# A second attention in thirteen phases beside a streaming projection, its second round moved behind a layer norm

## What is computed

```python
h = rms_norm(x, mix_norm_g)
q, kv, gate_logits, conv_in = split(h @ w_in_2)
gates = sigmoid(gate_logits)               # one for each head and branch
# three attentions: over 15 compressed blocks, over chosen blocks, over a window
p_cmp = masked_softmax(q @ k_cmp + bias_c); o_cmp = p_cmp @ v_cmp
p_sel = masked_softmax(q @ k_slc + bias_s); o_sel = p_sel @ v_slc
p_win = masked_softmax(q @ k_win + bias_w); o_win = p_win @ v_win
attn = gates[0] * o_cmp + gates[1] * o_sel + gates[2] * o_win   # 16 heads of 64
u = a * sigmoid(gate)                      # a, gate = split(conv_in)
conv = silu(layer_norm(causal_depthwise_conv(u, 31 taps)))      # 1024 channels
x = x + concatenate([attn, conv]) @ w_out_2
```

## Time and profile before

| | us |
|---|---|
| median of 3 runs | 2766.43 (2765.12 to 2769.42) |
| the profiled execution | 2766.32 |
| its span, first to last instruction | 2764.2 |
| TensorE busy | 2721.0 (98%) |
| DVE busy | 1945.6 (70%) |
| ACT busy | 1405.1 (51%) |
| mean granted TensorE clock | 0.994 |

### The profile page before, as it was taken

How to read it: one execution, slowest core, us unless ns; L and a number is a source line. 1 busy time by engine, 2 the same in 40 slices (tenths; PEclk the granted TensorE clock), 3 DMA queues, 4 the chain that set the end, 5 groups by cost and what they waited for, 6 DMA issues and landing times.

```text
span 2764.2 us, 41613 instructions
## 1 busy us (share of the span) xinstructions
PE 2721.0 (98%) x16606; PEld 2389.4 (86%) x16606; DVE 1945.6 (70%) x2922; ACT 1405.1 (51%) x2084; POOL 101.6 (4%) x189
## 2 busy tenths in 40 slices
PE   8999999999999999999999999999999999999998
PEld 7888888888888888888888899988888888888887
DVE  7448777757677775677656778876788775677764
ACT  6345555544455554455445551256655553455543
POOL 1320000000000000000000000000000000000000
PEclk9999999999999999999999999998999999999999
DMA  7457556555668878877656566862355555555554
GB/s 241 134 179 239 174 183 197 184 183 186 200 219 292 283 276 301 290 282 275 202 186 210 182 192 232 279 235 97 133 177 196 190 190 192 180 193 190 183 194 141
DMA packets 166609, 573.19 MB, mean 207 GB/s; under 512 B 19872, under 2 KB 26736, under 8 KB 165904
## 3 DMA queue, kind: packets, MB, share of 16 engines
q1 hardware_dynamic: 151216, 521.86, 56.6%
q0 software_dynamic: 15056, 48.65, 4.8%
q10 hardware_dynamic: 144, 0.01, 0.0%
HBM read 530.86 MB, written 38.90 MB: 206 GB/s over the span
## 4 chain that ended last, share of the span: by engine, by line
PE 90%; DVE 5%; ACT 2%; DMA 1%; issue 1%; POOL 0%; DVEq 0%; SPq 0%; ACTq 0%; POOLq 0%
PE PS L946 89%; DVE wl L1910 2%; DVE CC L1918 1%; DMA raw<-in_w_in 1%; ACT wh L1367 1%; PE PS L1282 0%; DVE H L1910 0%; DVE SQA L1910 0%; DMA XC<-KTC 0%; DVE QT L1910 0%; ACT TB L1367 0%; DMA raw<-in_w_up 0%; DVE Z L1910 0%; DVE RB L1969 0%; PE PS L1109 0%
## 5 line engine op out<-in xcount | busy, mean ns | idle before, releaser
L1910 DVE TENSOR_TENSOR wl<-raw,wh 128x1024 fp32r<-128x1024 f32 (+1 forms) x880 | 1029.8, 1195 | 442.9 <-ACT wh L1367 441.0
L1367 ACT ACTIVATE wh<-raw 128x1024 fp32r<-128x1024 f32 (+1 forms) x880 | 885.9, 1031 | 518.6 <-PE PS L946 418.5
L946 PE MATMUL PS<-CHt,wh 128*128 128x512 f32 x2816 | 886.1, 396 | 2.4 <-DVE wl L1910 2.4
L946 PE MATMUL PS<-BIGt,wh 128*128 128x512 f32 (+1 forms) x2816 | 758.5, 357 | 2.3 <-DVE wl L1910 1.3
L946 PEld LDWEIGHTS PS<-CHt,wl 128*128 128x128 f32 x2816 | 529.0, 188 | 124.8
L946 PE MATMUL PS<-AHt,wh 128*128 128x512 f32 (+1 forms) x1984 | 602.9, 385 | 12.6 <-DVE wl L1910 9.4
L946 PE MATMUL PS<-CHt,wl 128*128 128x256 f32 x2816 | 553.5, 278 | 0.0
L946 PEld LDWEIGHTS PS<-BIGt,wl 128*128 128x128 f32 x2304 | 436.6, 189 | 79.1 <-issue 0.2
L946 PE MATMUL PS<-BIGt,wl 128*128 128x256 f32 x2304 | 499.4, 280 | 0.0
L946 PEld LDWEIGHTS PS<-BIGt,wh 128*128 128x128 f32 x2816 | 436.9, 191 | 7.2 <-issue 4.7
L946 PEld LDWEIGHTS PS<-CHt,wh 128*128 128x128 f32 x2816 | 429.3, 189 | 2.9 <-issue 2.7
(11 more groups left out here) (307 smaller groups left out, 1648.3 us busy)
## 6 DMA issues: line engine op xcount, KB each, us to landing
raw<-in_w_up SPq DMA_DIRECT2D x264, 512.0 KB, 5.0
raw<-in_w_in SPq DMA_DIRECT2D x200, 512.0 KB, 4.1
raw<-in_w_down SPq DMA_DIRECT2D x132, 512.0 KB, 4.3
raw<-in_w_gate SPq DMA_DIRECT2D x88, 512.0 KB, 5.4
raw<-in_w_down SPq DMA_DIRECT2D x56, 384.0 KB, 3.6
raw<-in_w_ssd_br SPq DMA_DIRECT2D x32, 512.0 KB, 4.5
raw<-in_w_o SPq DMA_DIRECT2D x32, 512.0 KB, 4.3
PKR<-in_w_in SPq DMA_DIRECT2D x32, 512.0 KB, 5.1
```

The costliest lines, as they stand in the source:

```text
L946: return e.matmul(o, l, r, start=start, stop=stop, skip_group_check=True)
L1367: return e.activation(o, x, f, **k)
L1910: return e.tensor_tensor(o, x, y, op)
```

## The change

`ATTN2` gets thirteen phases for fifteen. `cmp` moves into the phase of `sc0`: the compressed scores are written beside the scores, to columns 384 to 413 of the same banks, and need no wait; DVE's `s0` waits for them and `ca` follows it in the same phase. The four scalings of a branch (`p0`, `p1`) move from ACT to DVE, into the phases `r0` and `r1`. The second round gets `AFTER_NORM` = 5 empty half pieces ahead of it. In `make_plan` a half piece in the middle may now also hold a norm phase back while bank 7 is taken.

```diff
-ATTN2 = dict(sc0=0, cmp=2, tr0=5, o0=6, sc1=7, trc=10, oc=12, tr1=12, o1=14, s0=0, ca=2, r0=2, cb=5, s1=7, r1=9,
-             out=14, e0=2, ce=3, p0=3, t0=5, e1=9, tc=10, p1=10, t1=12)
+ATTN2 = dict(sc0=0, cmp=0, tr0=4, o0=6, sc1=6, trc=8, oc=10, tr1=10, o1=12, s0=1, ca=1, r0=3, cb=4, s1=7, r1=9,
+             out=12, e0=2, ce=3, t0=5, e1=8, tc=8, t1=11)
+AFTER_NORM = 5
-BANK7 = (("sc0", "s0"), ("cmp", "ca"), ("tr0", "t0"), ("sc1", "s1"), ("trc", "tc"), ("tr1", "t1"))
+BANK7 = (("sc0", "ca"), ("tr0", "t0"), ("sc1", "s1"), ("trc", "tc"), ("tr1", "t1"))
...
-            add("w_in_2", 0, 16, 256 * i, "U2", "ev_q2", i,                 gens=[attn2_stage(2 * i, 0), attn2_stage(2 * i + 1, 2 if i == 0 else 0)], **k)
+            add("w_in_2", 0, 16, 256 * i, "U2", "ev_q2", i,                 gens=[attn2_stage(2 * i, AFTER_NORM if i == 1 else 0),
+                      attn2_stage(2 * i + 1, (2, AFTER_NORM + 2, 0, 0)[i])], **k)
...
-            if u.ev == "ev_add" or conv.live and conv.live[0][0] == "ln":
+            if u.ev == "ev_add" or conv.live and conv.live[0][0] == "ln" and not (
+                    len(conv.live[0][2]) > LN_END - 7 and bank7_taken()):
                 conv.step()
...
             if ph == ATTN2["cmp"]:
-                bank7("cmp")
-                e.wait_ge(d.sem, d.at(i, "n110"))
                 for b in range(2):
                     for hh in range(2):
-                        tok = mm(PS[:, S0 + hh, b * 15:(b + 1) * 15], Q2[hh * 64:hh * 64 + 64, t, b * P:(b + 1) * P],
+                        tok = mm(PS[:, S0 + hh, 384 + b * 15:384 + (b + 1) * 15], Q2[hh * 64:hh * 64 + 64, t, b * P:(b + 1) * P],
...
             if ph == ATTN2["tr0"]:
                 bank7("tr0")
-                e.wait_ge(ac.sem, ac.at(i, "p03"))
+                e.wait_ge(d.sem, d.at(i, "p03"))
...
-            def scale(br):
-                e.wait_ge(d.sem, d.at(i, f"rg{br}1"))
-                for hh in range(2):
-                    for b, c0, c1 in HALVES:
-                        x = SX[:, hh, c0:c1]
-                        af(x, x, ACT.Copy, scale=RC[:, hh, b:b + 1]).then_inc(ac.sem)
...
+                e.wait_ge(d.sem, d.at(i, f"rg{br}1"))
+                for hh in range(2):
+                    for b, c0, c1 in HALVES:
+                        x = SX[:, hh, c0:c1]
+                        ts(x, x, RC[:, hh, b:b + 1], None, MUL).then_inc(d.sem)
```

More of the change, by code:

```diff
@@ L709, in hybrid_block_kernel @@
     a2_d = [steps(f"attn2_d{u}", "n000", "n010", "n100", "n110", "cb0", "cb1", "cm", "cs0", "cs1", "cf", "rc0", "rg00",
[L710 to L713, removed]
+                  "rg01", *[f"p0{j}" for j in range(4)], "cd", "cr", "cc", "cg0", "cg1", "cx0", "cx1", "n001", "n011", "n101", "n111", "rc1", "rg10",
+                  "rg11", *[f"p1{j}" for j in range(4)]) for u in range(2)]
+    a2_a = [steps(f"attn2_a{u}", *[f"e0{i}" for i in range(4)], "ce", "pt0", *[f"e1{i}" for i in range(4)], "ptc", "pt1") for u in range(2)]
     add_d = steps("conv_half_added")
@@ L742, in hybrid_block_kernel @@
     RS2 = TA[:, 1, 0:2]
-    READ7 = {"sc0": (a2_d[1], "n110"), "cmp": (a2_d[1], "cb1"), "tr0": (a2_a[1], "pt0"), "sc1": (a2_d[1], "n111"),
+    READ7 = {"sc0": (a2_d[1], "cb1"), "tr0": (a2_a[1], "pt0"), "sc1": (a2_d[1], "n111"),
              "trc": (a2_a[1], "ptc"), "tr1": (a2_a[1], "pt1")}
@@ L1350, in attn2 @@
                 bank7("tr1")
-                e.wait_ge(ac.sem, ac.at(i, "p13"))
+                e.wait_ge(d.sem, d.at(i, "p13"))
                 turn()
@@ L1772, in attn2 @@
                 af(SC[:, :, :, :], SC[:, :, :, :], ACT.Exp).then_inc(ac.sem)
-            if ph == ATTN2["p0"]:
-                scale(0)
             if ph == ATTN2["t0"]:
@@ L1782, in attn2 @@
                 af(PT[0:15, :, 0:256], PS[0:15, S0:S0 + 2, 0:256], ACT.Copy).then_inc(ac.sem)
-            if ph == ATTN2["p1"]:
-                scale(1)
             if ph == ATTN2["t1"]:
@@ L2522, in scores @@
             def scores(br):
-                e.wait_ge(pe.sem, pe.at(i, f"sc{br}"))
+                e.wait_ge(pe.sem, pe.at(i, "sc1" if br else "cmp"))
                 if br == 0:
@@ L2555, in attn2 @@
                 for hh in range(2):
-                    tt(SC[:, hh, :, :], PS[:, S0 + hh, 0:30].rearrange("p (b n) -> p b n", b=2),
+                    tt(SC[:, hh, :, :], PS[:, S0 + hh, 384:414].rearrange("p (b n) -> p b n", b=2),
                        cb[:, :, :, 2 * t + hh], ADD).then_inc(d.sem)
```

## The result

| | before | changed |
|---|---|---|
| median (range), 6 executions each | 2765.38 us (2764.99 to 2769.42) | 2773.95 us (2773.58 to 2776.77) |
| ratio, 95% interval | | 1.0032 [1.0022, 1.0041] |
| profiled execution, its span | 2766.32, 2764.2 us | 2773.58, 2771.8 us |
| busy TensorE, DVE, ACT | 2721.0, 1945.6, 1405.1 us | 2720.2, 1960.3, 1381.9 us |

The changed kernel is slower by 0.32%, a little over the 0.2% that a measurement can tell. The forecast was 2772.5 us; the measured time lies 1.5 us above it, inside the range.

What follows compares the result with a forecast made beforehand. TensorE bounds the kernel, so only its stands and low-clock time, about 16 us in round two, can be won. Terms +3.7 - 3.7 + 3.2 + 3.0 = +6.2 us on 2766.32 gave 2772.5 us, range 2759.0 to 2779.5.

Steps and rivals of the forecast that it cites:

- round one: Half pieces h1 to h16, heads 0 and 1: DVE is behind and TensorE waits for it, +3.7 us.
- round two: Half pieces h17 to h36, heads 2 and 3: smaller norm gap and fewer stands, but head work still collides, -3.7 us.
- stands at head 1's transposes and at the compressed ones: Round one: TensorE waits 1.35 us for DVE's scaling at head 1's, 1.0 us at the compressed transposes.
- wait of head 3's scores for the norm's multiplies: Round two: head 3's first scores wait for bank 7, held by the norm; 3.1 us, and the clock falls.
- PT2a of head 2: Round two: lands at 1875.1 with TensorE ready at 1871.8; stand 3.3 us, and the clock falls again.
- The other side's rival: Round two: norm phases 8 and 9 pass early, so PT2a's stand goes; -6.6 us, 2759.7 in all; chance 0.25.
- Rounds three and four: Half pieces h36 to h64: DVE and ACT steps come late in fourteen half pieces; 3.2 and 3.0 us, +6.2 together.
- price of the scaling group: Four scalings on DVE taken as 0.7 us; 1.1 by the 410 ns row, about 4 us more in total.
- forecast sign of DVE being over 85% busy: Rounds three and four: 10-us stretches with DVE over 85% busy and TensorE stands under 1.1 us would show the forecast right.
- Step (a): Compressed scores written at once beside the scores: same matmuls, 0.5 us earlier; nothing by itself.
- slack suffices: Rival: rounds three and four and half of round one hide, the norm part as forecast; 2765.5 us; chance 0.20.
- none of the shorter stands is followed by the low level: Second attention before the change: only TensorE's stands of 1.96 us and more are followed by 1.2 GHz.

Runs made afterwards that it cites:

- e2: The changed kernel with AFTER_NORM = 0, so without the delay ahead of the second round; 2773.16 us.
- e7: The changed kernel with the first transposes, and the compressed part's transposes and copies, one half piece later each; 2769.54 us.
- e8: The kernel before with compressed scores at once behind the scores, and scalings on DVE only for heads 2 and 3; 2765.84 us.
- e4: The kernel before, fifteen phases kept, with only the compressed scores moved beside the scores, at once behind them; 2762.33 us.
- e12: The same kernel as e4 measured once more, against the kernel before; 2764.75 us, ratio 0.9990.
- e6: The changed kernel with only the first transposes one half piece later (phase 5 for 4); 2775.61 us.

## Why the prediction was right, and where it was not

| step | predicted | measured |
|---|---|---|
| round one | +3.7 | +4.0 |
| round two | -3.7 | -3.4 |
| round three | +3.2 | +3.8 |
| round four | +3.0 | +4.7 |
| outside the attention, and the remainder | 0 | -1.8 |
| profiled execution | 2772.5 | 2773.6 |

**Round one** has the sum right and its parts only in mixed form. The stands at head 1's transposes and at the compressed ones came as forecast, 1.56 us (1.35) and 0.95 (1.0). The first, forecast at 1.5, is 0.51: TensorE came 1.5 us late to it, since it ran at its low level from 1804 to 1807. In e2 the same round ran at the full level and the stand is 2.00; from the first scores to head 1's last values it took 37.34 us there and 37.33 here. DVE set this round's time, so a slow stretch of TensorE inside DVE's shadow cost nothing.

**Round two.** The norm's gap from its sums to its second matmul fell from 10.66 to 8.06 us (forecast 8.2). The wait of head 3's scores for the norm's multiplies is 2.98 us (3.1), and PT2a of head 2 came at 1875.74 (1875.1) with a stand of 2.70 (3.3). TensorE ran at the low level behind both, as said. It also did so from 1855 to 1858, behind the norm's stand of 0.85 us, which the forecast did not have; e7's trace has a stand of 0.86 us there and no such stretch. The other side's rival needed PT2a to end before 1872; it did not. The granted clock there, in the table of stretches:

```profile
1862.00:1864.00 2.00, 1.57 (x12) 1.41 (x12) 1.93 (x7) 1.05 (x3) 0.00 (x0) 0.50 0.02 8
...
1876.00:1878.00 2.00, 2.00 (x18) 1.67 (x18) 1.83 (x9) 2.00 (x7) 0.00 (x0) 0.50 0.03 8
```

**Rounds three and four** stood where they were said to stand, but for one place, and were mis-sized: 8.5 us for 6.2. Two terms failed. The first is the price of the scaling group, whose being well over 0.7 us was named as a sign of being wrong. The prediction worked out 0.7 us from the 290 ns row; it took 0.92. On the prediction's own scale, 4 us for 0.4 more, this makes some 2 us; no run varied the price alone. The scalings have a per-partition column as factor, and a row of just that form was in the same view of before, with one instruction; it had been passed over for the row with two:

```profile
L1914 DVE TENSOR_SCALAR RO<-RO,CV 128x256 f32<-128x256 f32 x1 | 0.4, 355 | 0.0
```

The second is that round four was taken as round three over again (3.0 for 3.2). The adds of w_out_2 come every four half pieces and a round has fourteen, so they lie at other places in it. In round three DVE's add came behind head 4's second scores, in round four it came ahead of head 6's:

```profile
1918.30 1.22 DVE L1899 TENSOR_TENSOR wl<-raw,wh 128x1024 fp32r<-128x1024 f32 x1
1919.43 0.28 DVE L2524 CUSTOM_DVE_ANT_0 SX2a<-PS,BM 128x128 f32<-128x128 f32 x1
...
1920.54 0.87 DVE L1907 SCALAR_TENSOR_TENSOR H<-H,CV,RXK 128x256 f32<-128x256 f32 x2
...
1954.17 0.88 DVE L1907 SCALAR_TENSOR_TENSOR H<-H,CV,RXK 128x256 f32<-128x256 f32 x2
...
1956.81 1.22 DVE L1899 TENSOR_TENSOR wl<-raw,wh 128x1024 fp32r<-128x1024 f32 x1
1957.95 0.28 DVE L2524 CUSTOM_DVE_ANT_0 SX2a<-PS,BM 128x128 f32<-128x128 f32 x1
```

So head 6's compressed transposes, which wait for those scores, stood 1.22 us, at a place where head 4's did not stand and the forecast had nothing. Other waits were smaller than forecast (0.45 us for 0.7 at PT2a in the second half). The forecast sign of DVE being over 85% busy in the 10-us stretches came in two of them only, 1910 (9.52) and 1940 (9.28); over the two rounds DVE was busy 27.7 and 28.0 us, the 28 that the prediction had counted, but that is 74% and 73% of them. The waits came from the order of its queue and not from its load.

Of the price: from 283 ns for 128 columns to 347 for 256 the slope is 0.5 ns per column, the rest some 220 ns per instruction. "VectorE: DVE Perf Modes" of the Trainium skill (the TRN2 errata section) says that SBUF-source instructions pay a fixed extra latency each, whatever their length; the two rows agree that most of such a small scaling is fixed. Its tier table, which the prediction used, was right on the rate (the squares of two tensors in e8's rows have a slope of 1.0 ns, from 0.43 us for 256 columns to 0.69 for 512); this fixed part is not in the table's multiples.

**Step (a), "nothing by itself", failed.** e4 and e12 give it 2.8 us, of which 1.9 are explained: the same matmuls were counted as the same cost, and the interruption of the stream around a short group (0.24 us for each head) was not. This hid inside the forecast: the other parts cost about 11 us together (2774.0 against 2763.1), not 6.2. Together with the -1.8 us outside the rounds, for which nothing was forecast, it is luck that the sum came within 1.5 us. The rival "slack suffices" was wrong in its core, since rounds three and four stood.

**The sentence that none of the shorter stands is followed by the low level** held for before's trace alone; the last section has counterexamples.

## What to carry to other kernels

Before work moves to an engine with idle time, ask what stands behind it in that engine's queue at each place: DVE was 70% busy, and two groups of scaling of 0.92 us ahead of the norm's squares cost TensorE 2 us of standing. A transpose and what reads it are one place: to shift one alone mostly hands the wait on. Where a round's length is no multiple of what runs beside it, each round is to be laid out by itself. And split a bundle before it is judged: one part of this one gains 0.1% alone, and what the delay wins in its round, the rounds that it pushes back return.

## What the runs showed of the hardware

The same stand of TensorE is followed by the low clock in one execution and not in another. e4 and e12 are one kernel. TensorE's timeline and the granted clock of the stretch behind it, in e4:

```profile
1802.39 0.93 PE L946 MATMUL PS<-KD,Q 64*128 64x128 f32 x8 [1.38 <-DVE Q L1916]
```

```profile
1804.00:1806.00 2.00, 2.00 (x12) 2.00 (x12) 2.00 (x11) 0.14 (x1) 0.00 (x0) 0.55 0.06 23
...
1856.00:1858.00 2.00, 1.67 (x19) 1.51 (x20) 1.25 (x9) 1.56 (x3) 0.00 (x0) 1.00 1.01 404
```

and in e12:

```profile
1801.75 0.93 PE L946 MATMUL PS<-KD,Q 64*128 64x128 f32 x8 [1.39 <-DVE Q L1916]
...
1854.21 0.99 PE L946 MATMUL PS<-M,SQA 128*128 128x1 f32 x4 [2.63 <-DVE SQA L1908]
```

```profile
1804.00:1806.00 2.00, 2.00 (x18) 1.89 (x16) 2.00 (x12) 0.79 (x3) 0.00 (x0) 1.00 0.25 37
...
1856.00:1858.00 2.00, 2.00 (x14) 1.67 (x11) 0.00 (x0) 0.00 (x0) 0.00 (x0) 0.50 1.00 399
```

Behind 1.38 us of standing the clock fell nearly to 1.2 GHz (0.55) in e4 and stayed at 2.4 in e12; with 2.62 and 2.63 us it was the other way round (in e12 it fell before the stand had ended). In the changed kernel's trace it fell to 0.50 behind its 1.38 us, in before's trace behind 1.39 us it did not. Between two kernels it is the same: the stands of 1.86 and 1.94 us in rounds three and four are followed by the low level in e6 and not in e7. "TensorE: Matmul & The Clock Gate" of the Trainium skill (Part 1: The HAM clock gate) says, of a kernel's start, that the same kernel measures a different number of slow matmuls from run to run; these traces show the like in the middle of one. So a stand has its own length as its sure price, and a further one with a chance: the stretches at the low level near a stand were some 3 to 7 us long in these traces (from 1804 to 1807 and from 1862 to 1868 in the changed kernel's), which at half speed is 2 to 3 us of TensorE's work. It costs nothing where another engine sets the time, as in round one of the changed kernel. The two profiled attentions of this one kernel differ by 2.1 us (161.6 and 163.6), and its executions spread over 6 us, which is why parts of 1 to 2 us could not be settled by medians.
